# A two-model decoder stack on one core: residual and output products with tokens on partitions

## What is computed

```python
def rmsnorm(x, g):                       # over the 1024 features of a token
    return x * rsqrt(mean(x * x, -1) + EPS) * g

for l in range(2):                       # first network
    y = mixer(rmsnorm(x, g[0]))          # "... @ w_out" at its end: product out0, out2
    x = x + rmsnorm(y, g[1])
    y = square(relu(rmsnorm(x, g[2]) @ w1)) @ w2          # out1, out3
    x = x + rmsnorm(y, g[3])

h = rmsnorm(x, norm_g) * (1 + scale) + shift              # second network
proj = h @ w_in
y_attn = (attn * silu(g_attn)) @ w_o_attn                 # out5
y_conv = (short_conv(cb, cc, cx, conv_w) * silu(g_conv)) @ w_o_conv   # out4
merged = sigmoid(m_attn) * y_attn + sigmoid(m_conv) * y_conv
x = x + gate * (merged @ w_out)                           # out6
return rmsnorm(x, final_g)
```

## Time and profile before

| | |
|---|---|
| median of 3 runs | 1113.49 us (1110.85 to 1114.81) |
| profiled execution: its span, first to last instruction | 1113.0 us |
| TensorE busy with matmuls, with weight loads | 1040.9 us (94%), 1028.0 us (92%) |
| VectorE, ScalarE, GpSimd busy | 665.1, 519.3, 464.2 us |
| mean granted TensorE clock | 0.955 of full speed |
| read from HBM | 182.75 MB, 165 GB/s over the span |

### The profile page before, as it was taken

The page is one execution under the profiler, slowest core; times in us unless marked ns, Lnnn a source line. Parts: engine busy times, 40 slices in busy tenths (PEclk is TensorE's granted clock), DMA queues, the critical chain, the costliest instruction groups (busy, mean ns, idle before and its releaser), DMA issues.

```text
span 1113.0 us, 18954 instructions
## 1 busy us (share of the span) xinstructions
PE 1040.9 (94%) x8250; PEld 1028.0 (92%) x8250; DVE 665.1 (60%) x729; ACT 519.3 (47%) x570; POOL 464.2 (42%) x160
## 2 busy tenths in 40 slices
PE   6988999789999997998879999998799999999997
PEld 5988999789999997998879999998799999999997
DVE  6899969567656646295557666754511366434244
ACT  6624474544443445454453444354444465434442
POOL 4546534643343444331352434344234334444541
PEclk8999999889999997897979999999799999999998
DMA  9743332616666772423243667675164654446520
GB/s 300 248 128 131 127 114 76 227 38 235 234 212 207 250 233 63 149 92 114 77 151 124 218 212 242 214 277 190 60 205 153 201 170 148 163 152 208 190 77 38
DMA packets 139238, 185.03 MB, mean 166 GB/s; under 512 B 4147, under 2 KB 124436, under 8 KB 139156
## 3 DMA queue, kind: packets, MB, share of 16 engines
q1 hardware_dynamic: 139140, 183.81, 49.9%
q10 hardware_dynamic: 16, 0.01, 0.0%
HBM read 182.75 MB, written 1.06 MB: 165 GB/s over the span
## 4 chain that ended last, share of the span: by engine, by line
PE 50%; DVE 3%; ACT 1%; issue 0%; ACTq 0%; DVEq 0%
PE bank L478 50%; DVE arena L881 1%; DVE work L881 1%; DVE work L884 0%; DVE gc L881 0%; PE bank L759 0%; DVE xT L881 0%; ACT arena L1423 0%; ACT wh L1430 0%; ACT L1423 0%; ACT work L1423 0%; ACT sd L1423 0%; PE bank L864 0%; ACTq L201 0%; ACT hh L1423 0%
## 5 line engine op out<-in xcount | busy, mean ns | idle before, releaser
L1716 POOL TENSOR_TENSOR wl<-raw,wh 128x2048 fp32r<-128x2048 f32 x78 | 367.5, 4712 | 479.4 <-ACT wh L1430 452.4
L478 PE MATMUL bank<-hh,wh 128*128 128x256 f32 x1440 | 412.4, 295 | 8.8 <-ACT hh L1423 6.7
L478 PE MATMUL bank<-hl,wh 128*128 128x256 f32 x1440 | 402.9, 286 | 2.5 <-POOL hl L1725 2.5
L881 DVE TENSOR_TENSOR wl<-raw,wh 128x2048 fp32r<-128x2048 f32 x80 | 262.4, 3280 | 237.5 <-ACT wh L1430 182.7
L478 PE MATMUL bank<-hh,wl 128*128 128x256 f32 x1440 | 402.4, 287 | 0.2 <-DVE wl L881 0.2
L1430 ACT CAST wh<-raw 128x2048 fp32r<-128x2048 f32 x158 | 299.0, 1903 | 139.3 <-PE bank L478 137.3
L478 PEld LDWEIGHTS bank<-hh,wh 128*128 128x128 f32 x1440 | 280.9, 200 | 10.1 <-issue 9.8
L478 PEld LDWEIGHTS bank<-hl,wh 128*128 128x128 f32 x1440 | 276.1, 194 | 4.3 <-POOL hl L1725 4.1
L478 PEld LDWEIGHTS bank<-hh,wl 128*128 128x128 f32 x1440 | 277.0, 196 | 0.5 <-DVE wl L881 0.5
L478 PE MATMUL bank<-yh,wh 128*128 128x256 f32 x864 | 245.3, 284 | 3.4 <-ACT wh L1430 3.4
L478 PE MATMUL bank<-yl,wh 128*128 128x256 f32 x864 | 245.2, 284 | 0.0
(11 more groups left out here) (167 smaller groups left out, 989.7 us busy)
## 6 DMA issues: line engine op xcount, KB each, us to landing
raw<-in_mlp_w SPq DMA_DIRECT2D x64, 1024.0 KB, 5.5
raw<-in_w_in SPq DMA_DIRECT2D x40, 1024.0 KB, 5.2
raw<-in_ev_w_in SPq DMA_DIRECT2D x20, 1024.0 KB, 5.3
raw<-in_w_ada SPq DMA_DIRECT2D x12, 1024.0 KB, 5.2
raw<-in_od_w_in SPq DMA_DIRECT2D x12, 1024.0 KB, 5.7
raw<-in_ev_w_out SPq DMA_DIRECT2D x6, 1024.0 KB, 5.0
raw<-in_od_w_out SPq DMA_DIRECT2D x4, 1024.0 KB, 4.9
raw<-in_w_o_conv SPq DMA_DIRECT2D x4, 1024.0 KB, 4.9
```

Of the source, the lines that this page charges most:

```text
L478: return eng.matmul(o, l, r, start=start, stop=stop, skip_group_check=True)
L881: return eng.tensor_tensor(o, x, y, op)
L1716: eng.tensor_tensor(wl[:, u % RING, :], raw[:, u % RING, :], wh[:, u % RING, :].bitcast(F32), ALU.subtract).then_inc(S["lo_pool"], 1)
```

## The change

- All B units run with tokens on partitions: the stationary operand is 128 tokens of `yh` or `yl`, and 512 weight columns move. A unit is 24 matmuls in place of 48 (`b_part`). Units `mc` and `ma` take the form T too.
- The last two units of `out0`, `out1`, `out2`, `out3` and `out5` are run together (`b_end`): all of both for tokens 0 to 127, then for tokens 128 to 255. While they run no unit is split; the two splits left out come after the norm (`splits_at`).
- The residual `x` has tokens on partitions. The norms take their sums along the free dimension on ScalarE (`squares`, with its accumulator), token half by token half; the gain of a post-norm comes as a row spread over partitions by a DMA (`grow`). TensorE then transposes the residual for each norm (`x_turn`, 16 transposes), and ScalarE and VectorE read `hh` and `hl` out of PSUM. GpSimd has no part in the norms any more.
- `out5`'s merge is done on rows, then transposed (`merged_turn`), and `out6` runs all four units for the first 128 tokens and then for the rest (`b_last`). The final norm needs no transposes; the gate comes as a row through DRAM; four DMAs of 256 KB write the result.
- In `a_first` the low weights are waited for ahead of the first matmul.

Cut to its core, TensorE's part first (to `x_turn`), then VectorE's:

```diff
+ENDS = {last_of(f"out{p}"): p for p in (0, 1, 2, 3, 5)}
+def splits_at(u):
+    if u in ENDS:
+        return []
+    return [s for s in ([u + AHEAD - 1] if u - 1 in ENDS else []) + [u + AHEAD] if 0 <= s < NU]
...
-                for j, k in enumerate(x_tiles(norm)):
-                    eng.wait_ge(S["hh"], KT * norm + j + 1)
-                    both(w_hi, hh, k, first=j == 0)
                 wait_low(eng, u)
-                for k in x_tiles(norm):
+                for k in range(KT):
+                    eng.wait_ge(S["hh"], KT * norm + k + 1)
+                    both(w_hi, hh, k, first=k == 0)
                     both(w_lo, hh, k)
...
+            def b_part(u, t, half, first, last):
+                for k in range(2):
+                    y_hi, y_lo = yh[:, kt + k, t * P:(t + 1) * P], yl[:, kt + k, t * P:(t + 1) * P]
+                    mm(acc(t, half)[:, :], y_hi, w_hi[:, k, half_of(half)], first and k == 0, False)
+                    mm(acc(t, half)[:, :], y_hi, w_lo[:, k, half_of(half)], False, False)
+                    m = mm(acc(t, half)[:, :], y_lo, w_hi[:, k, half_of(half)], False, last and k == 1)
...
+            def b_end(u):
+                for t in range(TT):
+                    for half in range(2):
+                        m = b_part(u - 1, t, half, False, False)
+                        m = b_part(u, t, half, False, True)
...
+            def b_last():
+                for t in range(TT):
+                    merged_turn(t)
+                    eng.wait_ge(S["yl6"], 2 * t + 2)
+                    for pair in range(2 if t == 0 else 1):
+                        units = range(first + 2 * pair, first + 2 * pair + 2) if t == 0 else range(first, NU)
+...
+                        for half in range(2):
+                            for u in units:
+                                m = b_part(u, t, half, u == first, u == NU - 1)
...
+            def x_turn(n):
+                for t in range(TT):
+                    for k in range(KT):
+                        if n in LATE:
+                            if k % 4 == 0:
+                                eng.wait_ge(S["x_n"], 4 * (n - 1) + 2 * t + k // 4 + 1)
+                        elif k == 0:
+                            eng.wait_ge(S["x_w"], (2 if n == 4 else 0) + t + 1)
+                        m = eng.transpose(x_bank(n, k)[:, t * P:(t + 1) * P], src[:, t, k * P:(k + 1) * P], ident[:, :])
...
             def prenorm(n):
+                if n in (0, 4):
+                    for t in range(TT):
+                        link(eng.reciprocal(rs[:, t:t + 1], sd[:, t:t + 1]))
+                        ts(work_t[:, t, :], x[:, t, :], rs[:, t:t + 1], None, ALU.mult).then_inc(S["x_w"], 1)
+                for k in range(KT):
+                    if n == 4:
+                        ts(h_shift[:, k, :], x_bank(n, k), gain(n, k), mod[:, k:k + 1], ALU.mult, ALU.add)
+                        tt(hl[:, k, :], h_shift[:, k, :], hh[:, k, :].bitcast(F32), ALU.subtract)
+                    else:
+                        stt(hl[:, k, :], x_bank(n, k), gain(n, k), hh[:, k, :].bitcast(F32), ALU.mult, ALU.subtract)
+                if n == 2:
+                    for k in range(KT):
+                        ts(work[:, k, :], x_bank(n, k), gain(n, k), None, ALU.mult).then_inc(S["wk"], 1)
...
             def postnorm(n):
+                for t in range(TT):
+                    for half in range(2):
+                        eng.wait_ge(S["ysq"], 4 * n + 2 * t + half + 1)
+                        m = tt(yg[:, t, half_of(half)], acc(t, half)[:, :], grow[:, half_of(half)], ALU.mult)
+                    eng.wait_ge(S["ysd"], 2 * n + t + 1)
+                    link(eng.reciprocal(rs[:, 2 + t:3 + t], sd[:, 2 + t:3 + t]))
+                    for half in range(2):
+                        stt(x[:, t, half_of(half)], yg[:, t, half_of(half)], rs[:, 2 + t:3 + t],
+                            x[:, t, half_of(half)], ALU.mult, ALU.add).then_inc(S["x_n"], 1)
...
+                if u == at("out6"):
+                    merge(0)
+                    merged_low(0)
+                    merge(1)
                 before(u)
+                for s in splits_at(u):
...
+                if u == at("out6"):
+                    merged_low(1)
...
+            for t in range(TT):
+                for half in range(2):
+                    link(tt(fin_p[:, t, c], acc(t, half)[:, :], fin_gate[:, c], ALU.mult))
+                    tt(x[:, t, c], x[:, t, c], fin_p[:, t, c], ALU.add).then_inc(S["fin_x"], 1)
+                link(eng.reciprocal(rs[:, 8 + t:9 + t], sd[:, 10 + t:11 + t]))
+                for half in range(2):
+                    stt(fin_t[:, t, c], x[:, t, c], rs[:, 8 + t:9 + t], fin_gain[:, c], ALU.mult, ALU.mult)
```

More of the change, by code:

```diff
@@ L557, in column_sums @@
-            def column_sums(stat_col, tiles, first=True, last=True):
-                for sq in tiles:
-                    for tt in range(TT):
-                        m = mm(PS[2][:, stat_col + tt:stat_col + tt + 1], sq[:, tt * P:(tt + 1) * P], ones[:, :],
-                               first and sq is tiles[0] and tt == 0, last and sq is tiles[-1])
-                return m
+            def b_part(u, t, half, first, last):
+                role, i = UNITS[u][3:]
+                w_hi, w_lo = slot(wh, u, "B"), slot(wl, u, "B")
+                kt = 2 * i if PHASE[role] not in (1, 3) else 2 * (i % 4)
+                for k in range(2):
[3 more added lines that the diff above has]
+                    m = mm(acc(t, half)[:, :], y_lo, w_hi[:, k, half_of(half)], False, last and k == 1)
+                return m
@@ L913, in gain @@
                 return gs[:, g:g + 1]
-            def fold(sq, order, done, n, out):
-                first = pair_of(sq, order[0])
-                eng.wait_ge(done, 4 * n + 1)
-                for j in range(1, 4):
-                    eng.wait_ge(done, 4 * n + j + 1)
-                    link(tt(first, first, pair_of(sq, order[j]), ALU.add))
-                tt(first[:, 0:SEQ], first[:, 0:SEQ], first[:, SEQ:2 * SEQ], ALU.add).then_inc(out, 1)
             def x_root(n):
-                eng.wait_ge(S["xsd"], n + 1)
-                eng.reciprocal(rs[:, 0:2], sd[:, 0:2]).then_inc(S["xrs"], 1)
+                eng.wait_ge(S["x_sd"], n + 2)
@@ new lines, in prenorm @@
+                if n in (0, 4):
+                    for t in range(TT):
+                        if n == 0:
+                            eng.wait_ge((S["d_x0"], S["d_x1"])[t], 16)
+                        else:
+                            eng.wait_ge(S["x_n"], 4 * (n - 1) + 2 * t + 2)
+                        squares(junk_x[:, t, :], x[:, t, :], 4 + t, S["x_ssq"])
+                        eng.wait_ge(S["x_ssq"], 2 * n + t + 1)
+                        root(sd[:, t:t + 1], st[:, 4 + t:5 + t], D).then_inc(S["x_sd"], 1)
@@ L1583, in _ @@
                     prenorm(n + 1)
-                if u + AHEAD in SPLIT_OF and u + AHEAD >= 2:
-                    high(u + AHEAD)
+                if u == at("out6"):
+                    merged_high(0)
+                for s in splits_at(u):
+                    if s in SPLIT_OF and s >= 2:
+                        high(s)
+                if u == at("out6"):
+                    merged_high(1)
                 if PRENORM.get(u) in LATE:
@@ L1754, in _ @@
                                           scr1[:, j % 2, :].rearrange("p (h t) -> p h t", h=2), ALU.mult).then_inc(S["k"], 1)
-                if u == last_of("out5"):
-                    for j in range(4):
-                        y_low(6, j)
-                s = u + AHEAD
-                if s < NU and split_by(s) == "pool":
-                    split(s)
+                for s in splits_at(u):
+                    if split_by(s) == "pool":
+                        split(s)
                 if u < 0:
```

466 lines of the change are left out of this document (194 added, 272 removed).

## The result

The changed kernel takes 1081.3 us (median of four runs, 1080.96 to 1088.7; of another five, 1080.6 to 1088.0), the one before 1114.2 us beside it: ratio 0.972, interval 0.970 to 0.975. It is 33 us faster; the forecast had said 53, and 1081.3 lies just above its range. The profiled execution spans 1079.0 us.

What follows compares the result with a forecast made beforehand. PE was taken to bind the MLPs by matmul distance, and chains to bind norms and ends. Savings 27.6 + 9.4 + 8.5 + 8.3 + 5.9 - 6.8 = 52.9 from 1113.5 gave 1061 us; own range 1052 to 1069, overall 1046 to 1080.

Steps and rivals of the forecast that it cites:

- Part 1: B units: 24 matmuls of 512 columns replace 48 of 256, saving 0.576 us per unit, 27.6 us over 48.
- I take 0.216: B streams: 512-column matmuls start every 0.216 us, the extra 13 ns being a weight-load floor that vanishes behind longer streams.
- The bound 0.227: B streams: the 13 ns belong to each matmul, so 512 columns take 0.227 us; 48 units then save 15 us.
- the first rival: B streams: 512-column matmuls keep the extra, 0.227 or 0.240 us each; 1075 or 1092 us in all; chance 0.13.
- the slower and the no-change case: 512 weight columns stream slower in B units, 1149 to 1330 us, chance 0.03; or nothing changes, chance 0.01.
- The MLPs can give it: MLPs: splits and low parts need some 19 us per turn of five units, which shrinks from 23.0 to 21.9.
- the rival of new waits: Phase ends: paired units and splits make PE wait, 2 to 4 us at each of five ends; 1071 to 1081; chance 0.16.
- the forecast's 0.56: Chance given to the main forecast of 1061 us, whose own range is 1052 to 1069.
- Parts 2 and 3: Norms 1 to 3 save 9.4, 8.5 and 8.3 us through shorter chains; norm 4 saves 5.9.
- Part 4: `out6` takes 9.0 us more through waits for transposes and splits, the end gives 2.2 back: net loss 6.8.
- Part 5: Start: first matmuls from about 18.8 instead of 14.7 us, then unbroken; net zero, between 1 gained and 2 lost.

Runs made afterwards that it cites:

- e3_yl_first: Changed kernel with VectorE making the last hidden low part ahead of the last weight unit's split at each MLP's end; 1079.3 us, ratio 0.968.
- e2_no_ends: Changed kernel without the paired last units and put-off splits, each residual phase running its units one after the other; 1077.1 us, ratio 0.967.
- e4_root_first: Changed kernel with ScalarE's squares between its two postponed casts and VectorE's reciprocal ahead of its split behind norms 1 to 3; 1075.4 us, ratio 0.964.
- e6_pool_late: Changed kernel with GpSimd's split behind norm 4 waiting until all eight hl tiles are made; 1082.6 us, ratio 0.970.
- m1_streams: Computation left out, bare matmul streams on TensorE alone: rounded f32 at 256, 384 and 512 columns started every 0.121, 0.174 and 0.227 us.
- e5_low_last: Changed kernel with the products of the low weights last in the very first unit; 1085.1 us, one run of six at 1079.0, ratio 0.973.

## Why the prediction was wrong

**Part 1, the size of its term.** The step that failed is "I take 0.216". The 512-column matmul starts every 0.227 us, and a B unit saves 0.307 us, not 0.576: 14.7 us for 48 units, 12.9 less. The rows behind it were real, but none was a rounded-f32 stream at the high clock; the earlier trace rows, the only one that was, said 13 ns, and it held. The bound 0.227 was named, and it was the first rival; its price with the other parts as forecast, 1075, was too low as well. The range to 1080 took the rivals one at a time, and two of them came together. The chances hold a slip: all but the slower and the no-change case add up to 0.96, not 0.95.

**Part 1, its cover.** "The MLPs can give it" was checked by throughput, not by order. At both MLP ends PE waits 2.18 us, because the two last units are taken together and a low part stands behind a split and then beside GpSimd's (shown by `e3_yl_first`, and by `e2_no_ends`, where the units are taken one by one and the waits are gone). With nine matmuls of 0.43 in place of 0.23 us behind the first wait, 6 us. This is the rival of new waits, at two of its five ends. I had put the forecast's 0.56 on neither happening; both did. In `out0` three units' gain, not two's, ended in the wait for `wh`, which grew from 3.35 to 4.28 us; behind it 12 matmuls of 512 columns ran at the low clock in place of 17 of 256, which lost 2.4 us in place of 1.6.

**Parts 2 and 3, right.** Norms 1 to 3 take 14.9 from last squares to spread (forecast 15.4), with the split on VectorE ending 2.15 behind GpSimd's (forecast 2.3) and the reciprocal behind it; `e4_root_first` shows that this link was the last one and could be taken away. The low clock that I had put at the head of the first unit did not come (1.00 in norm 3), so that PE stands 2.39 us there, not 1.9. Norm 4 to the first `aq` read takes 759.90 - 740.29 = 19.6 (forecast 19.1), with the gap among the last `hl`; `e6_pool_late` shows whose it was. The Trainium skill, "SBUF — State Buffer", "Who interferes with whom", has a VectorE instruction with two SBUF inputs and a GpSimd instruction that reads SBUF exclude each other: the rows shown agree (0.42 against 4.21, 0.69 against 4.40 and 5.05 us).

**Part 4, right in its waits, its size in part by luck.** `out6` lengthened by 7.4 (forecast 9.0), its two `yl` waits are 1.56 each, that for `wl` 2.86 (forecast 3.9). The 1.5 us of low clock behind that wait did not come, and 96 matmuls at 0.227 instead of 0.216 took 1.0 more: two misses that nearly cancel. The end takes 6.8 (forecast 7.6).

**Part 5, wrong by 2 us at the place, by 1 in the end.** The first matmul came at 20.35, not 18.8: with `x` loaded first, `ident` and the small rows land at 7.28 instead of 4.66, and VectorE has its first reciprocal behind the copies that need them, at 10.36. The second unit starts 2.2 late, of which 1.3 come back as it no longer starts at the low clock.

**The sum.** Forecast 52.9; the matmul's distance takes 12.9 off, the streams' other losses 7.5, the start 2.2; norms, `out6` and end add 3.7 over forecast (0.5 for each of norms 1 to 3, -0.3, 1.6, 0.8): 34.0, and 1113.0 - 1079.0 is 34.0. Of the 7.5, the two MLP stages hold 7.9: the two waits, the 1.8 us of low clock behind the first, and 1.6 in the second, where 17 matmuls, from 1.5 us behind the start of norm 3's spread on, run at 0.21 us instead of 0.12. `aq` to `out5` is 1.0 short: `aq`'s second unit starts with nine matmuls at 0.21 us, behind the wait for `hl`, where it started at 0.12 before, which is 0.8 of it. The stage of `out2` is 1.3 better than by count.

## What to carry to other kernels

Take the price of a new shape from a row of the same data type at the same clock, and if there is none, let the bounds stand rather than the row that fits best. When work becomes due in pairs, or splits are put off, check each queue's order at that point, not only each engine's throughput: here a VectorE instruction with two SBUF inputs that was due just behind the start of a GpSimd split came out only after the split's end (0.69 became 5.05 us). And judge a change of structure only when the orders around it have been set for it: the same ends cost 4 us with the one set of orders and brought 10 with the other. Read gains of under some 5 us from the stages of the trace, not from the medians.

## What was not expected of the hardware

A rounded-f32 matmul costs 14 ns over its columns at the high clock from 256 to 512 columns, whether the stationary operand changes or not; plain f32 2.5 ns per record of 1024 column times (`m1_streams`). At 128 columns a rounded-f32 matmul takes 0.11 us, twice the 0.053 of its columns.

The same instructions can run at another mean clock in another execution. In a stretch of 51 us from norm 2 on (419 to 470) the profiles of the changed kernel, of its repetition and of `e6_pool_late` show a granted clock of 0.97, that of `e5_low_last` 0.87, though none of the edits touches it; the stage takes 138.5 and 141.5 us. Of nine runs of the unaltered changed kernel seven lay within 1.1 us of each other and two were 7 us slower. What decides between the levels was not found, and no profile shows one of the two slower runs.
